# Attention steps in pairs behind whole projection units, in a two-layer decoder trunk

## What is computed

```python
proj = h @ w_in_even[i]                       # ga, gb: the gates; qa, ka, va: attention
...
score = jnp.where(s_pos[None, None, :] <= t[None, :, None], score, -jnp.inf)
_, sel = lax.top_k(score, top_k)              # 128 keys for each query
...
logits = jnp.einsum('bqhd,bqkhd->bhqk', qa, ks).astype(jnp.float32) * scale
logits = logits + jnp.transpose(bias, (0, 3, 1, 2))
logits = jnp.where(valid[:, None, :, :], logits, -jnp.inf)
p = jax.nn.softmax(logits, axis=-1).astype(vs.dtype)
o = jnp.einsum('bhqk,bqkhd->bqhd', p, vs)
...
o_a = o_a.reshape(B, S, A_W) * jax.nn.silu(ga)
...
o_b = o_b.reshape(B, S, B_VW) * jax.nn.silu(gb)
x = x + jnp.concatenate([o_a, o_b], axis=-1) @ w_out_even[i]
```

## Time and profile before

| what | value |
|---|---|
| runs of the kernel before | 535.61, 536.95 (median), 538.23 us |
| profiled execution | 536.27 us |
| its span | 534.5 us |
| mean granted TensorE clock | 0.997 of full speed |
| TensorE matmuls busy | 517.4 us, 97% |
| VectorE busy | 376.9 us, 71% |
| GpSimd busy | 291.2 us, 54% |
| ScalarE busy | 236.2 us, 44% |
| share of TensorE in the chain that ended last | 78% |

### The profile page before, as it was taken

The page is one execution under the profiler, slowest core; times in us unless marked ns, Lnnn a source line. Parts: engine busy times, 40 slices in busy tenths (PEclk is TensorE's granted clock), DMA queues, the critical chain, the costliest instruction groups (busy, mean ns, idle before and its releaser), DMA issues.

```text
span 534.5 us, 7512 instructions
## 1 busy us (share of the span) xinstructions
PE 517.4 (97%) x2806; PEld 415.2 (78%) x2806; DVE 376.9 (71%) x772; ACT 236.2 (44%) x370; POOL 291.2 (54%) x180
## 2 busy tenths in 40 slices
PE   7799999999999899999999999999999999999995
PEld 6775788777777778888898889877777777777883
DVE  3895499859966455657471146799989999969825
ACT  6433843233121154453371345266555564257413
POOL 4380455755734047646506314689999999342701
PEclk9999999999999999999999999999999999999998
DMA  8524256222222002010082321612222222402004
GB/s 262 169 71 140 63 175 198 78 80 80 78 80 80 0 1 80 4 77 1 6 309 80 100 58 46 193 38 79 80 78 78 80 78 80 157 0 80 1 0 158
DMA packets 43642, 46.75 MB, mean 87 GB/s; under 512 B 4432, under 2 KB 32107, under 8 KB 43606
## 3 DMA queue, kind: packets, MB, share of 16 engines
q1 hardware_dynamic: 43606, 46.28, 27.4%
HBM read 44.03 MB, written 2.12 MB: 86 GB/s over the span
## 4 chain that ended last, share of the span: by engine, by line
PE 78%; DVE 14%; issue 3%; ACT 2%; DMA 1%; POOL 1%; SPq 0%; POOLq 0%; ACTq 0%; DVEq 0%
PE bank L1506 28%; PE bank L1526 28%; PE bank L1808 3%; PE bank L1650 3%; PE bank L1718 3%; DVE r_va L1068 2%; PE bank L1695 2%; DVE top L1066 2%; PE bank L1796 2%; PE bank L1707 2%; DMA r_x<-in_x_dram 1%; DVE r_vb L1017 1%; DVE r_ob L1052 1%; PE bank L1814 1%; DVE level_mask L1018 1%
## 5 line engine op out<-in xcount | busy, mean ns | idle before, releaser
L532 POOL TENSOR_TENSOR w_lo<-w_raw,w_hi 128x2048 fp32r<-128x2048 f32 (+1 forms) x31 | 140.3, 4527 | 94.6 <-ACT w_hi L681 93.6
L1506 PE MATMUL bank<-hT_hi,w_hi 128*128 128x512 f32 (+1 forms) x280 | 112.6, 402 | 0.8 <-POOL w_lo L532 0.8
L1506 PE MATMUL bank<-hT_hi,w_lo 128*128 128x512 f32 (+1 forms) x280 | 111.0, 397 | 0.0
L1506 PE MATMUL bank<-hT_lo,w_hi 128*128 128x512 f32 (+1 forms) x280 | 111.0, 396 | 0.0
L1526 PE MATMUL bank<-w_hi,hT_hi 128*128 128x512 f32 x252 | 102.6, 407 | 0.1
L1526 PE MATMUL bank<-w_hi,hT_lo 128*128 128x512 f32 x252 | 98.5, 391 | 0.0
L1526 PE MATMUL bank<-w_lo,hT_hi 128*128 128x512 f32 x252 | 98.4, 390 | 0.0
L681 ACT ACTIVATE w_hi<-w_raw 128x2048 fp32r<-128x2048 f32 (+1 forms) x35 | 65.7, 1879 | 39.6 <-PE bank L1526 37.0
L1324 DVE SCALAR_TENSOR_TENSOR bank<-r_va,pvec,bank 128x512 f32<-128x512 f32 x108 | 76.0, 747 | 0.9
L618 POOL TENSOR_TENSOR r_g<-r_g 128x512 f32<-128x512 f32 x48 | 62.0, 1291 | 11.2 <-ACT r_g L862 5.5
L1506 PEld LDWEIGHTS bank<-hT_hi,w_hi 128*128 128x128 f32 (+1 forms) x280 | 52.3, 187 | 14.5 <-issue 2.6
(11 more groups left out here) (226 smaller groups left out, 792.9 us busy)
## 6 DMA issues: line engine op xcount, KB each, us to landing
w_raw<-in_w_in_even_dram SPq DMA_DIRECT2D x14, 1024.0 KB, 5.2
w_raw<-in_w_in_odd_dram SPq DMA_DIRECT2D x16, 512.0 KB, 4.7
w_raw<-in_w_out_even_dram SPq DMA_DIRECT2D x4, 1024.0 KB, 8.5
w_raw<-in_w_in_odd_dram SPq DMA_DIRECT2D x4, 1024.0 KB, 5.1
w_raw<-in_w_out_odd_dram SPq DMA_DIRECT2D x4, 1024.0 KB, 5.0
r_x<-in_x_dram SPq DMA_DIRECT2D x4, 512.0 KB, 6.1
r_x<-bias_rows SPq DMA_DIRECT2D x4, 512.0 KB, 6.2
r_x<-in_x_dram SPq DMA_DIRECT2D x1, 2048.0 KB, 8.0
```

The lines of the kernel that those rows point to most:

```text
L532: nc.gpsimd.tensor_tensor(v(w_lo[j % 3]), v(w_raw[j % 2]), v(w_hi[j % 3]).bitcast(F32), ALU.subtract).then_inc(lo_ready, 1)
L1506: ins = nc.tensor.matmul(proj_bank(g)[0:m, :], w[:, k, P * i:P * i + m], h[:, k, :], start=(n == 0), stop=(n == 3 * KC - 1))
```

## The change

TensorE's order in slots 12 to 15 is written anew. Every unit from r = 1 on issues its twelve products in one run. Behind them stand `prob_transpose(2r - 1)`, `qk_pair(2r + 2)`, `pv(2r - 2)`, `prob_transpose(2r)` and `pv(2r - 1)`. Unit 0 stays in two halves with `qk_pair(0)` between. Behind the last unit the order is that of `attend(31)` and `pv(31)`, written out. The queues of the other engines, the waits inside each piece and the buffers are as they were.

```diff
--- before.py
+++ after.py
@@ -1719,10 +1719,17 @@
                                            va[:, i, AD * h:AD * h + AD], start=(i == 0), stop=(i == tb))
                 ins.then_inc(pv_done, 1)
 
-            def attend(n):
-                prob_transpose(n)
-                if n:
-                    pv(n - 1)
+            def steps_behind_unit(r):
+
+                if r:
+                    prob_transpose(2 * r - 1)
+                if 2 * r + 2 < NSTEP:
+                    qk_pair(2 * r + 2)
+                if r:
+                    pv(2 * r - 2)
+                prob_transpose(2 * r)
+                if r:
+                    pv(2 * r - 1)
 
             for s_ in range(3, S_OE):
                 slot_ready(s_)
@@ -1739,16 +1746,16 @@
                             outputs_b(t)
                 else:
                     for t in range(TB):
-                        for half in range(2):
-                            n = AH * (s_ - ATT_S0) + 2 * t + half - 1
-                            if half and 0 < n < NSTEP - 2:
-                                qk_pair(n + 2)
-                            unit_b(s_, t, part=(2 * half, 2 * half + 2))
-                            if n <= 0:
-                                qk_pair(2 * n + 2)
-                            if n >= 0:
-                                attend(n)
-            attend(NSTEP - 1)
+                        r = TB * (s_ - ATT_S0) + t
+                        if r == 0:
+                            unit_b(s_, t, part=(0, 2))
+                            qk_pair(0)
+                            unit_b(s_, t, part=(2, 4))
+                        else:
+                            unit_b(s_, t)
+                        steps_behind_unit(r)
+            prob_transpose(NSTEP - 1)
+            pv(NSTEP - 2)
             pv(NSTEP - 1)
 
             pe.wait_ge(act_emptied, evacs_through(FIRST[S_OE] - 1, "act"))
```

## The result

The changed kernel takes 540.04 us (median of 12 runs, 538.45 to 541.66), the kernel before beside it 536.83 us (12 runs, 535.61 to 538.69). The ratio is 1.006, with a 95% interval from 1.0044 to 1.0075: slower by 0.6%, 3.2 us. That is in the stated range (535.6 to 541.5), 1.6 us above the likeliest case (538.4), and on the slower side of the 0.5% bound, to which I had given 3 in 10. The profiled execution has a span of 538.3 us and a mean granted clock of 0.992.

A forecast was written before the change was run, and what follows sets the result against it. TensorE, busy for 97% of the span, was taken as the bound. Terms -0.4 + 1.36 + 0.5 = +1.5 us on a median of 536.95 gave 538.4 us, with an 8-in-10 range of 535.6 to 541.5.

The forecast's parts named there:

- likeliest case: Whole kernel: ScalarE's piece at step 18 and the tail cost more than merged runs save; 538.4 us, chance 0.5.
- 0.5% bound: About 2.7 us, what a measurement can tell from no change; slower beyond it had chance 0.3.
- TensorE's account: Units 1 to 15: merged runs of twelve products save slightly more than new changes of kind cost; -0.4 us.
- Bank 6: Second transposes wait for VectorE's copy from the shared bank: costed at nothing, 0.95 us to spare; as rival 545, chance 0.08.
- The wait at step 18: Step 18's transposes wait for ScalarE's exponential, since step 15's transposes release its long piece later; +1.36 us.
- The end: End of the stage: later last Silu and VectorE gate products start the next stage 0.5 us later, bounds 0.1 and 0.9.
- The clock: At the step 18 wait: granted clock taken to stay at 1.00, so no cost beyond the standstill.
- changes of kind: Rival: in every unit, TensorE's switches between kinds of matmul cost the upper bound, +2.7 us; total 541.5, chance 0.2.
- Nothing was faster: Rival: merged runs save at the lower bound or more and step 18 is not held; 534.3 us, chance 0.1.

The follow-up runs named there:

- e8_before_split: The kernel before, with only the split of weight slot 16 moved behind ScalarE's exponentials of steps 18 and 19: 537.5 us, ratio 1.0003.
- e7_tail_old: The changed kernel with slot 16's split behind the exponentials of steps 18 and 19, and unit 15 in the old two halves: 536.88 us, ratio 1.0006.
- e9_logits_first: The changed kernel with slot 16's split behind the exponentials of steps 18 and 19, and the logits pair ahead of both transposes: 541.5 us, ratio 1.0091.
- e1_split_later: The changed kernel with the split of weight slot 16 moved behind ScalarE's exponentials of steps 18 and 19: 537.0 us, ratio to before 1.0008.
- e4_unit8_old: The changed kernel with unit 8 alone in the old order of two halves: 537.16 us, ratio 1.001.
- e2_warm: The changed kernel with 13 small bfloat16 matmuls in TensorE's wait ahead of the transposes of step 18: 537.72 us, ratio 1.0021.

## Why the prediction was right in range and too low

- **TensorE's account** (-0.4): -0.28 is what remains of the difference between the stages, and 0.15 us is gained between `e8_before_split` and `e7_tail_old`. The run of twelve takes 2.86 instead of 2.83. PV behind QK costs 0.94 - 0.81 = 0.13 over PV into products, close to the 0.15 of the earlier trace rows. Transposes into QK, which I took as PV into QK is now (0.93 where PV into products takes 0.81, so 0.12), cost 0.53 - 0.44 = 0.09. A full-width unit takes 6.65 instead of 6.68 (264.72 - 258.04 in the trace of before) and gains 0.03, where I had 0.02. Right.
- **Bank 6** (nothing, with 0.95 us to spare): right, no unit with logits between its transposes has a wait there; and that the logits are the cover is shown by `e9_logits_first`.
- **The wait at step 18** (+1.36): measured +1.40, at the place and for the reason given, with the chain of 8.77 us unchanged; shown by `e1_split_later` and `e4_unit8_old`, which take it away from its two ends.
- **The end** (+0.5): measured +0.44, with 0.23 us of wait ahead of the transposes of step 30 where I had 0.1, and VectorE behind the Silu as described. The traces of `e7_tail_old` and `e1_split_later`, without and with it, differ by 0.38; their medians, 536.88 and 537.0, can't tell it.
- **The clock**: this is the step that failed, in one sentence: "The granted clock there is 1.00, and I take it to stay." I had worked out 1.52 us of standstill for an engine that had not stood still in the stage before, and priced only the standstill. It measured 1.57 us in unit 10, as much as the wait itself, and 538.4 + 1.6 is the 540.0 that came. With it in the sum the forecast would have been slower and not within 0.5%. Shown by `e2_warm` (same order, same wait, filled in part: no fall) and by `e1_split_later` (same order, no wait: no fall). That it is as large as the wait is chance as far as these runs show. The Trainium skill describes such a loss (TensorE: Matmul & The Clock Gate, "HAM oscillation — how this bites in real kernels"): waits for data between bursts of matmuls let the clock fall, and the next burst starts cold. The trace of the changed kernel agrees in kind, with 2.85 us of products taking 4.42; but the waits of that page are of 3 to 5 us behind short bursts, and one of 1.41 us amid full work is not its case.
- The rivals: changes of kind did not cost 0.20 a unit, so 541.5 had the right side for a wrong reason. The range reached as far as it did only by that rival, so that it holds the measured 540.0 is in part luck. Bank 6 did not wait. Nothing was faster.

What stays open: whether the new order makes the clock fall at a shorter wait than the old. In the old order 12 runs show no sign of a fall at 1.36 us, in the new one it fell at 1.41 in nearly all; but the clock held in the trace with 1.25 us in the new order and in the one with 1.70 us in the old. No run has the same idle time in both orders. A limit is shown for neither.

## What to carry to other kernels

A transfer of work past a wait must be followed to the engine that the moved instruction releases: here an odd step's transposes came 1.4 us later, with no effect in thirteen units; in unit 15 it cost 0.4 us at the end, and in unit 8 they released the one long piece in ScalarE's queue (two table loads, a Silu and a split). Where such a piece stands between two steps, look for what in it can be moved behind the exponential that TensorE waits for; moving one split was worth the whole loss. And if a change makes TensorE stand still at a place where it was busy all the time, work out the price with a fall of the clock and without: here a wait of 1.41 us brought another 1.57 us in nearly all runs, and waits up to 1.36 us brought no fall that the runs show.

## What the runs showed of the hardware

- The granted clock fell behind a single wait of TensorE amid otherwise full work, to the lower of its two levels (1.2 GHz; products 0.42 us apart instead of 0.23). In the traces it fell behind an idle time of 1.41 us (new order) and 2.52 us (old order), and held behind 0.68, 0.73, 1.07 and 1.25 us (new) and 1.36 and 1.70 us (old). The mean clock of 12 runs each (6 for the last two) is 0.9947, 0.9942, 0.9933, 0.9928 and, in the old order, 0.9939 at 1.36 us, all about those of the kernels without the wait (0.9929 to 0.9942); 0.9910 at 1.41 us in the new order; 0.9917 at 1.70 us and 0.9887 at 2.52 us in the old.
- The same wait does not always bring it. Near the start TensorE waits for VectorE until 20.5 us: 2.49 us in the trace of before, where the clock stayed at 1.00 behind it, and 2.48 us in that of the changed kernel, where it was 0.66 from 20 to 25 us.
- A wait is not needed for it either. Between 475 and 490 us the clock fell in five traces (0.75 and lower in the 5 us with the lowest clock), with no wait of TensorE above 0.1 us in the 25 us ahead; what stands there among the products are groups of eight matmuls of one column.
- The mean clock sorts the runs of the kernel before into levels: beside the first group of experiments, those with 0.997 had a median of 535.63 us, with 0.994 of 536.65, with 0.991 of 538.59. Differences of under a microsecond are better read from stretches of the traces than from medians.
- 128x128 bfloat16 matmuls in a row took 0.89 us for 13 in a wait, where at the kernel's start 36 of them take 4.00; I had taken the latter. Why they differ is not shown.
- Transposes into a group of 64 rows cost 0.09 us over transposes into values products.
